# The delta net's triangular inverse on one Trainium2 core: one matrix grown by products, its transpose taken on TensorE

## What is computed

```python
a_mat = jnp.where(strict, jnp.einsum('bhncd,bhnsd->bhncs', kb, k) * gamma, 0.0)
t_mat = lax.linalg.triangular_solve(eye + a_mat, jnp.broadcast_to(eye, a_mat.shape),
                                    left_side=True, lower=True, unit_diagonal=True)
u = jnp.einsum('bhncs,bhnsv->bhncv', t_mat, v * beta[..., None])
w = jnp.einsum('bhncs,bhnsk->bhnck', t_mat, kb * jnp.exp(gc)[..., None])
```

## Time and profile before

| what | value |
|---|---|
| median of 3 runs | 1892.87 us (1889.32 to 1898.02) |
| profiled execution, its own time | 1896.64 us |
| its span, first to last instruction | 1894.8 us |
| granted TensorE clock, mean | 0.985 of 2.4 GHz |
| PE, DVE, ACT, POOL busy | 96%, 89%, 66%, 5% |
| read from HBM | 531.5 MB, 282 GB/s over the span |

### The profile page before, as it was taken

One profiled execution on the slowest core, in us unless ns is written; L12 is line 12 of the kernel. 1 busy time (PEld: TensorE's weight loads), 2 busy tenths in 40 slices (PEclk: granted clock), 3 DMA queues, 4 the chain that ended last, 5 costly groups with the idle time before them and its releaser, 6 DMA issues.

```text
span 1894.8 us, 33593 instructions
## 1 busy us (share of the span) xinstructions
PE 1827.1 (96%) x13102; PEld 1709.5 (90%) x13102; DVE 1682.1 (89%) x2239; ACT 1246.4 (66%) x1963; POOL 94.6 (5%) x72
## 2 busy tenths in 40 slices
PE   6999999999999998999999999999899999999998
PEld 5889899999998898989998997999789889988997
DVE  7888997977898799999999898899898979998896
ACT  6667754744665675656666676866577867667783
POOL 0000031031000001122000000000000000000000
PEclk9999998999999998999999999999999999999999
DMA  8887876868999896889899997888789878877995
GB/s 289 263 291 245 289 235 223 299 211 280 308 361 334 296 312 234 277 292 310 291 323 339 338 321 244 298 270 259 238 286 325 276 245 315 249 268 247 336 313 181
DMA packets 258523, 535.81 MB, mean 283 GB/s; under 512 B 23608, under 2 KB 28733, under 8 KB 257341
## 3 DMA queue, kind: packets, MB, share of 16 engines
q1 hardware_dynamic: 257933, 531.44, 82.8%
q10 hardware_dynamic: 432, 2.23, 0.3%
HBM read 531.50 MB, written 2.10 MB: 282 GB/s over the span
## 4 chain that ended last, share of the span: by engine, by line
PE 45%; DVE 14%; issue 3%; ACT 2%; DMA 1%; DVEq 0%; ACTq 0%
PE ps L152 44%; DVE ring_r L1954 5%; DVE AR_r L1954 2%; DVE macc L1954 1%; DVE AR L1946 1%; DVE stg L1954 1%; DMA ring<-in_w_in 1%; ACT w L1500 1%; DVE stg L1946 1%; DVE AR L1954 1%; ACT stg L1506 1%; ACT AR L1500 0%; DVE AR L2435 0%; DMA ring<-in_w_out 0%; DVE sm L2431 0%
## 5 line engine op out<-in xcount | busy, mean ns | idle before, releaser
L1954 DVE SCALAR_TENSOR_TENSOR ring_r<-ring,w 128x1024 fp32r<-128x1024 f32 x483 | 585.3, 1234 | 79.6 <-ACT w L1500 78.0
L1500 ACT ACTIVATE w<-ring 128x1024 fp32r<-128x1024 f32 x483 | 500.8, 1057 | 179.8 <-PE ps L152 80.2
L152 PE MATMUL ps<-hh_r,w 128*128 128x256 f32 x3480 | 503.4, 288 | 2.7 <-DVE hlo L1954 2.4
L152 PEld LDWEIGHTS ps<-hh_r,w 128*128 128x128 f32 x3480 | 451.1, 191 | 11.0 <-issue 8.1
L152 PE MATMUL ps<-hlo,ring_r 128*128 128x256 f32 x3108 | 435.4, 283 | 0.1
L152 PEld LDWEIGHTS ps<-hlo,ring_r 128*128 128x128 f32 x3108 | 399.1, 189 | 0.5 <-DVE ring_r L1954 0.5
L1954 DVE SCALAR_TENSOR_TENSOR AR_r<-AR,w 128x1024 fp32r<-128x1024 f32 x146 | 177.7, 1231 | 27.1 <-ACT w L1500 26.7
L152 PE MATMUL ps<-AR 128*128 128x64 f32 (+5 forms) x1320 | 180.0, 296 | 12.3 <-DVE AR L1950 6.1
L152 PEld LDWEIGHTS ps<-AR 128*128 128x128 f32 (+1 forms) x1320 | 163.3, 195 | 21.7 <-issue 11.9
L1500 ACT ACTIVATE w<-AR 128x1024 fp32r<-128x1024 f32 x146 | 152.3, 1057 | 45.7 <-PE ps L152 19.0
L1954 DVE SCALAR_TENSOR_TENSOR macc<-ring,sm,macc 128x1024 f32<-128x1024 f32 x135 | 176.6, 1308 | 1.0 <-DMA ring<-in_w_mod 0.5
(11 more groups left out here) (226 smaller groups left out, 2222.8 us busy)
## 6 DMA issues: line engine op xcount, KB each, us to landing
ring<-in_w_in SPq DMA_DIRECT2D x313, 512.0 KB, 5.1
ring<-in_w_mod SPq DMA_DIRECT2D x145, 512.0 KB, 5.6
ring<-in_w_up SPq DMA_DIRECT2D x124, 512.0 KB, 5.4
ring<-in_w_out SPq DMA_DIRECT2D x66, 512.0 KB, 5.6
ring<-in_w_down SPq DMA_DIRECT2D x66, 512.0 KB, 6.1
AR<-in_w_in SPq DMA_DIRECT2D x64, 512.0 KB, 5.7
AR<-in_w_up SPq DMA_DIRECT2D x52, 512.0 KB, 5.6
AR<-in_w_mod SPq DMA_DIRECT2D x34, 512.0 KB, 5.1
```

The source lines that it names most:

```text
L152: return e.matmul(o, l, x, start=start, stop=stop, skip_group_check=True)
L1500: return e.activation(o, i, ACT.Copy, scale=scale)
L1954: return e.scalar_tensor_tensor(o, a, s, b, op0, op1)
```

## The change

The inverse `XX` is no longer grown by a product of its own. A level has three segments, `pp`, `xt` and `tx`, except the last, which has no `tx`:

- `pp` is as before, but waits for ACT's copy of `XX` instead of DVE's subtraction;
- `xt` has only the four matmuls for `XT`, and DVE only that subtraction;
- `tx` is new: TensorE transposes the four matrices `XT` whole, after DVE's subtraction, and ACT copies every second block of w times 2 columns into `XX`.

Per job that removes 20 matmuls of 64 columns and 5 subtractions of 128 by 256, and adds 20 transposes of 128 by 128 and 5 copies of 128 by 256. POOL clears `PP` and masks `AL` at the same events as before. The job has 33 segments instead of 28; the pauses of levels are (2, 1, 1) instead of (2, 2), and the chain keeps its length in chunks. The pauses of other jobs and the shifts of modulation chunks are set anew beside that.

```diff
+def level(seg):
+
+    if 6 <= seg <= 22:
+        return (seg - 3) // 3, (seg - 6) % 3, -1
+    return 0, 0, seg if seg < 6 else seg - 5
...
-    "z": (0, 1), "gdn": (2, 1, 1, 1, 2) + 14 * (2,) + (1, 1, 1, 1, 1, 4, 1, 1), "merge": (0, 0, 1, 1),
+    "z": (0, 1), "gdn": (2, 1, 1, 1, 2, 2) + 5 * (2, 1, 1) + (2, 2, 2) + (1, 1, 1, 1, 1, 4, 1, 1), "merge": (0, 0, 1, 1),
...
-    ('convq', 'q', 3): (0, 1, 1, 3, 2, 1),
+    ('convq', 'q', 2): (0, 1, 1, 6, 0, 1), ('convq', 'q', 3): (4, 1, 1, 3, 2, 1),
...
-MODS = {19: -2, 42: -2, 48: -1, 64: -3, 70: -2, 78: 1, 90: -3, 92: -3, 93: -4, 94: 3, 104: -2, 107: 4, 123: 3,
-        124: 3, 134: 2, 140: 3, 154: -2, 160: -1, 166: 2, 172: -1, 185: 3}
+MODS = {17: -1, 19: -2, 21: 4, 22: 2, 42: -2, 47: -1, 48: -1, 64: -3, 70: -2, 78: 1, 87: 3, 89: 1, 90: -3, 91: -1,
+        92: -3, 93: -4, 94: 3, 104: -2, 107: 4, 122: -3, 123: -1, 124: 3, 134: 2, 140: 3, 141: 2, 150: 4, 151: 2,
+        154: -2, 158: 2, 160: -1, 166: 2, 170: 2, 172: -1, 178: 2, 185: 3}
...
-                else:
-                    e.wait_ge(*gdn_act.after(f"pp{l}", bt))
-                    for u in range(4):
-                        q = fp(blocked(a[:, 64 * u:64 * u + 64], w), G.PP[:, u, :], halfway(G.XT[:, u, :], 1, w))
-                    if l < 6:
-                        for u in range(4):
-                            q = fp(blocked(a[:, 256 + 64 * u:320 + 64 * u], w), G.XT[:, u, :], halfway(G.PP[:, u, :], 0, w))
-                    q.then_inc(*gdn_pe.step(f"xt{l}", bt))
+            if l > 0 and part == 1:
+                e.wait_ge(*gdn_act.after(f"pp{l}", bt))
+                for u in range(4):
+                    q = fp(blocked(a[:, 64 * u:64 * u + 64], w), G.PP[:, u, :], halfway(G.XT[:, u, :], 1, w))
+                q.then_inc(*gdn_pe.step(f"xt{l}", bt))
+            if part == 2:
+                e.wait_ge(*gdn_dve.after(f"xt{l}", bt))
+                for u in range(4):
+                    q = e.transpose(quarter(a, u), G.XT[:, u, :], ident)
+                q.then_inc(*gdn_pe.step(f"tx{l}", bt))
...
+            if part == 2:
+                e.wait_ge(*gdn_pe.after(f"tx{l}", bt))
+                copy(halfway(flat2(G.XX), 0, 2 * w), halfway(a[:, :], 0, 2 * w)).then_inc(*gdn_act.step(f"xx{l}", bt))
...
-                XT1, XX0 = halfway(flat2(G.XT), 1, w), halfway(flat2(G.XX), 0, w)
+                XT1 = halfway(flat2(G.XT), 1, w)
                 tt(XT1, XT1, blocked(a[:, 0:256], w), SUB).then_inc(*gdn_dve.step(f"xt{l}", bt))
-                if l < 6:
-                    tt(XX0, XX0, blocked(a[:, 256:512], w), SUB).then_inc(*gdn_dve.step(f"xx{l}", bt))
```

More of the change, by code:

```diff
@@ L179 @@
[L179 to L183, removed]
@@ L184 @@
-    ('sparse', 0, 1): (2, 3, 1, 4, 3, 1), ('sparse', 0, 3): (5, 1, 0, 5, 3, 1), ('sparse', 1, 0): (1, 1, 3, 2, 2, 2),
[3 rows of a table added]
+    ('gdn', 0): (2, 1, 1, 1, 3, 2, 2, 1, 1, 2, 1, 1, 2, 1, 1, 2, 1, 1, 2, 1, 1, 2, 2, 2, 1, 1, 1, 1, 1, 4, 1, 1),
+    ('gdn', 2): (2, 1, 1, 1, 2, 1, 2, 1, 1, 2, 1, 1, 2, 1, 1, 2, 1, 1, 2, 1, 1, 2, 2, 2, 1, 1, 1, 1, 1, 4, 1, 1),
+    ('indexer', 1): (1, 1, 1, 1, 1, 1, 1, 4, 2, 1, 1, 1, 1), ('kn', 1): (0, 0, 2, 1),
+    ('moba', 2): (2, 0, 1, 4, 2, 1, 1), ('modend', 0, 2): (2,), ('modend', 1, 0): (8,), ('modend', 1, 1): (4,),
@@ new lines @@
+    ('modend', 1, 2): (7,), ('modend', 1, 3): (7,), ('modend', 1, 4): (7,), ('modend', 1, 5): (7,),
+    ('qn', 1, 0): (0, 2, 2, 1), ('retain', 0, 0): (2, 2, 4, 3, 4, 1, 1), ('retain', 0, 1): (5, 2, 2, 3, 4, 1, 1),
+    ('retain', 0, 2): (5, 1, 2, 3, 4, 1, 1), ('retain', 0, 3): (4, 2, 2, 3, 5, 0, 1),
+    ('retain', 1, 0): (4, 2, 4, 1, 3, 1, 2), ('retain', 1, 2): (4, 2, 4, 3, 4, 1, 1),
+    ('retain', 1, 3): (4, 5, 2, 1, 6, 1, 1), ('setup',): (2, 2, 0, 1, 1), ('sparse', 0, 0): (1, 1, 1, 3, 4, 0),
@@ L214 @@
             "+a +b -a@gdn_act.vb3 -b@gdn_act.kx3", "+a -a@gdn_act.xx",
[L215 to L216 removed]
+            *[s for l in range(1, 7) for s in (f"+a -a@gdn_act.pp{l}", f"+a -a@gdn_dve.xt{l}", f"+a -a@gdn_act.xx{l}")][:-1],
             "+a +b -a@gdn_act.vn -b@gdn_act.wt", "+a -a@gdn_act.ss", "+a +b -a@gdn_act.qs1 -b@gdn_dve.v1",
@@ L1275, in gdn @@
             bt, = J.at
+            l, part, seg = level(seg)
+            w = 1 << l
             G = Gdn(bt)
@@ L1727, in gdn @@
                 copy(flat2(G.XX), a[:, :]).then_inc(*gdn_act.step("xx", bt))
-            if 6 <= seg <= 17 and seg % 2 == 0:
-                l = (seg - 4) // 2
-                w = 1 << l
+            if l > 0 and part == 0:
                 e.wait_ge(*gdn_pe.after(f"pp{l}", bt))
@@ L2582, in gdn @@
                 tt(G.AL, G.AT, mid(lev[:, 1, :], 4), MUL).then_inc(*gdn_pool.step("al1", bt))
-            if seg == 5 or (seg % 2 == 1 and 7 <= seg <= 15):
-                l = (seg - 3) // 2
-                if l > 1:
-                    e.wait_ge(*gdn_pe.after(f"xt{l - 1}", bt))
-                e.memset(flat2(G.PP), 0.0).then_inc(*gdn_pool.step(f"zero{l}", bt))
-            if 6 <= seg <= 14 and seg % 2 == 0:
-                l = (seg - 4) // 2
+            if seg == 5:
+                e.memset(flat2(G.PP), 0.0).then_inc(*gdn_pool.step("zero1", bt))
+            if 0 < l < 6 and part == 0:
                 e.wait_ge(*gdn_pe.after(f"pp{l}", bt))
                 tt(G.AL, G.AT, mid(lev[:, l + 1, :], 4), MUL).then_inc(*gdn_pool.step(f"al{l + 1}", bt))
+            if 0 < l < 6 and part == 1:
+                e.wait_ge(*gdn_pe.after(f"xt{l}", bt))
+                e.memset(flat2(G.PP), 0.0).then_inc(*gdn_pool.step(f"zero{l + 1}", bt))
         def bias_in(J, seg):
```

31 lines of the change are left out of this document (11 added, 20 removed), and 2 rows, old and new, of the table PLACES.

## The result

The changed kernel takes 1874.79 us in the median of 4 runs (1873.74 to 1876.17). With a fourth run the kernel before has a median of 1895.44 us. The ratio is 0.9893 with a 95% interval of [0.9872, 0.9914], so the time is 1.1% shorter. The profiled execution took 1876.17 us, 20.5 less than that of before, and its span 1874.4. Of all executions in this document one is left out of every figure as slow: 2201.89 us at a mean granted clock of 0.75, in the second series of the kernel with job 0 set apart.

The account below looks back on a forecast made before the run. TensorE (PE) was taken to bound the inverse's stretch, with gaps and low clock elsewhere. Terms -10 + 3 - 5 - 2 - 0.3 - 1.3 - 4.1 - 1.3 + 3.6 = -17.4 gave a 1875.5 us median, range 1868 to 1889.

Parts of the forecast that it names:

- PE's exchange, -10: In the inverse, TensorE drops product matmuls (-17.8 us), gains transposes (+7.2) and costlier interruptions (+0.7); taken as -10 us.
- The new wait, +3: In the inverse, `tx` waits for DVE's late subtraction, seven counted in both job pairs; +3 us, between 0 and +8.
- Segments 3 and 4, -2: Jobs 0 and 1 go in step and modulation chunks come later, so three gaps of 3.4 us shrink; -2 us.
- The slow stretch, -5: Around the second `modend` at 294 us, moving both `convq` sums away keeps the clock up; -5 us, or 0.
- The third `modend`, -0.3: At 380 us, sum and last modulation chunk both move one place ahead, so nearly all the wait moves along; -0.3 us.
- The second block's first layer, -1.8: Stretch from 1198.72 to 1450.64 us: `vb(0, 0)` -1.3, `sparse (0, 0)` +3.6 and `retain (0, 1)` -4.1; together -1.8 us.
- +3.6 for the earlier `sparse (0, 0)`: Segment 4 arrives a chunk earlier, so PE's 1.32 us wait becomes about 3.2, plus 1.7 for low clock; +3.6 us.
- `retain (0, 1)`, -4.1: Segment 1 in the second block: the 2.52 us gap and 1.6 us of slow records behind it go; -4.1 us.
- the first (the clock still falls at 294 us): Thin work around the second `modend` still lowers the clock, so -12.4 us in all: 1880.5 us; chance 0.20.
- The second (the gaps don't go away, they move): Gap cuts in the second block and first stretch are paid back elsewhere; -3 to -8, about 1887 us; chance 0.17.
- The third needed DVE late at most of the `tx`: The wait at `tx` takes the gain, +10 to +15 us instead of +3: 1883 to 1890 us; chance 0.12.
- The fourth needed low clock at the `tx` waits: Waits at `tx` pull the clock down, costing 4 to 7 us each; slower, 1905 us; chance 0.06.

Follow-up runs that it names:

- the kernels with the new pauses: The changed kernel and one with the old inverse but all other jobs' new pauses: 1874.79 and 1877.68 us, repeated side by side 1875.20 and 1876.51 us.
- the second profile: The changed kernel, unaltered, run once more beside the one with the old inverse and new pauses: median 1875.20 us, ratio 0.9889.
- whichever half stood alone: Against the kernel before: only the new inverse with its own pauses, 1890.15 us; or only the other jobs' new pauses and modulation shifts, 1877.68 us.

## Why the prediction was right, and where it wasn't

The median came 0.7 us from the forecast, and that is luck: the profiled executions differ by 20.5 us where the sum had 17.4, and three runs of before had a median 2.6 us below that of four. Step by step:

- **PE's exchange, -10: right in kind, somewhat large.** The work in the stretch fell by 8.1 us, and by 8.4 and 9.1 between the kernels with the new pauses. Apart it is 16.5 us for the product, where the sum had 17.8, and 7.5 for the transposes, where it had 7.2. The Trainium skill's price, 22 us for the transposes, was wrong for this kernel, as the rows of four had said.
- **DVE and ACT at nothing: right for ACT,** whose 20 copies cost no idle time of PE that the trace shows. For DVE the cover held too, except where the next two points say.
- **The new wait, +3: right** at 3.3 us (2.3 in the second profile), at three or four of the 20 `tx`.
- **Segments 3 and 4, -2: wrong.** They cost +1.4 us in this profile: gaps of 3.1 instead of 3.4 us, and 1.7 lost in the slow groups behind them. The step that failed is the one that had PE gain what DVE's list gains. DVE scales the matrices of both jobs back to back, 2.15 us each, and PE stands for both in turn. Setting the jobs apart halved these gaps, and the next waits took it back.
- **The slow stretch, -5: right in its size, wrong in its reason.** It went in the profile after, but the crowd of one-column sums doesn't decide the clock there: 0.72 before, then 1.00, 0.92 or 0.91 in kernels and profiles with and without it. What the pauses of `convq` do bring is 3 us of waits at `tx`. What makes the clock fall in one execution and not in the next stays open.
- **The third `modend`, -0.3: right in the wait, without the clock.** The wait of 1.3 us is gone and one of 0.85 us stands at the transposes of line 1309 behind it. The low clock behind the old wait (382.5 to 385.9 us, 1.7 us lost) is gone too, and the prediction had no term for it. It took a gap of 1.63 us as too short for a fall, while this one of 1.27 in the same trace had one.
- **The second block's first layer, -1.8: mis-sized, -5.6.** Ahead of the sum of `macc` the forecast was -1.3 + 3.6 = +2.3, and -3.5 was measured. DVE's chain of `vb(0, 0)` did lose one modulation chunk, 1.3 us. But the prediction added +3.6 for the earlier `sparse (0, 0)` beside it, as if the two waits were independent. They are two waits of one lagging engine: the 1.9 us that PE waits more at 1294 us it waits less at 1330. The gap there fell by 4.0 us, and with it the slow groups, which the prediction had not counted: in the kernel before PE is busy for 3.8 us between 1342 and 1348 us, all at a clock of 0.50, so about 1.9 us. The term of +3.6 was really about -1: the layer takes 247.6 and 247.0 us in the two kernels with the sparse job's old pauses, and 246.3 in the changed kernel.
- **`retain (0, 1)`, -4.1: right at its place, half of it at the end of the layer.** The gap of 2.52 us and the slow records behind it are gone. Behind the sum of `macc` the layer is only 2.1 us shorter, as two new waits of 0.22 and 0.77 us stand at 1396 and 1420 us; the other 1.1 us are not accounted for.
- **`retain (1, 0)`, -1.3: right** at 1.2 (2.15 to 0.92), and four smaller waits behind it shrank by 1.4 us, which makes most of the -3.1 of the stretch.
- **Not forecast**: 1.8 us between 648 and 1199 us. PE's wait at 733 us is 5.31 instead of 5.87 and two of 0.2 us are gone; the rest is not accounted for.

Of the rivals, the first (the clock still falls at 294 us) came true by a third in the changed kernel's second profile, where 1.7 us are lost from 291.0 to 294.4 us. The second (the gaps don't go away, they move) holds for the first block and for the sparse job, where most of the gap time that an edit closed came back a few chunks on. It doesn't hold for the second block as a whole, where DVE's list itself got shorter ahead of what PE waits for. The third needed DVE late at most of the `tx`, and three or four of 20 waited. The fourth needed low clock at the `tx` waits. The longest, 2.05 us, had none behind it in the changed kernel, but the same wait of 2.04 us had one with `convq`'s old pauses, at a cost of 1.7 us and not 4 to 7.

A sum of parts was the wrong form in one respect. It treats the work taken off PE, the idle time and the clock as if none answered to the others. The work did add. Some of it came back as waits, 2.0 to 5.2 us of 8.4 to 9.1, and the low clock was lost or won once, in whichever half stood alone.

## What to carry to other kernels

Where one engine lags behind another, all the waits for it in that stretch are one quantity: here an edit that lengthened one wait and left the lagging engine's list alone cost nothing at the end, and what gained was cutting that list ahead of the awaited step. Before adding up gains on the busiest engine, count with waits that come back; here 2.0 to 5.2 us of the 8.4 to 9.1 us of instructions did. And take a difference between two profiles apart into idle time, time at low clock and the rest before giving it a cause: an edit's own part is the one that comes again in a second profile. Price a transposing or small matmul from start to start in a row of its own kind, not from its length.

## What the runs showed of the hardware

The same program showed a granted clock of 1.00 over 288 to 306 us in one profile and 0.92 over 284 to 306 in another. In the 40 us ahead the only difference in PE's gaps was one of 0.38 us at a `tx`. The length of the low clock differs too: 10.2 us in the kernel before (293.8 to 304.0 us), 3.4 in the changed kernel's second profile (291.0 to 294.4).

The length of a single gap didn't decide it either. Behind the wait of 2.05 us at a `tx` the clock held in the changed kernel, and behind the same wait of 2.04 us it fell with `convq`'s old pauses and held in the kernel with job 0 apart and the sparse job's old pauses (445.02 us). Behind the gap of `vb(0, 0)` it fell at 2.58 and 2.73 and held at six lengths from 2.57 to 2.70 us. It fell behind all nine gaps of 3.21 or 3.22 us at `sparse (0, 0)` and behind that of 5.26, and also behind one of 1.27 us (380.94 us, before) and two of 1.43 and 1.22 us close together (233.96 and 236.25).

Four float32 transposes of 128 by 128 in a row took TensorE 0.36 to 0.38 us from start to start and eight 0.80, so 0.1 us each, while the length of one record was 0.275 us.
